# A second gate and up pair as seven products in seven of the FFNs, spread over the down stage

## The reference

```python
def swiglu(x, w_gate, w_up, w_down):
    return (jax.nn.silu(x @ w_gate) * (x @ w_up)) @ w_down
```

## Time and profile before

| | us |
|---|---|
| median of 3 runs | 2436.98 (2436.88 to 2441.23) |
| profiled execution | 2436.97 |
| its span | 2435.2 |
| PE busy | 2407.2 (99%), 12606 matmuls |
| VectorE busy | 1710.7 (70%) |
| ScalarE busy | 1255.4 (52%) |

### The profile page before, as it was taken

One profiled execution on the slowest core, in us unless ns is written; L12 is line 12 of the kernel. 1 busy time (PEld: TensorE's weight loads), 2 busy tenths in 40 slices (PEclk: granted clock), 3 DMA queues, 4 the chain that ended last, 5 costly groups with the idle time before them and its releaser, 6 DMA issues.

```text
span 2435.2 us, 30841 instructions
## 1 busy us (share of the span) xinstructions
PE 2407.2 (99%) x12606; PEld 2053.7 (84%) x12606; DVE 1710.7 (70%) x1755; ACT 1255.4 (52%) x1367; POOL 205.5 (8%) x358
## 2 busy tenths in 40 slices
PE   8999999999999999999999999999999999999998
PEld 6889998888889988888889878888888898778887
DVE  6555867857866778768658657777687677577884
ACT  5435545535537545445435664555455356645552
POOL 0100200101100100100100010001001000100010
PEclk9999999999999999999999999999999999999999
DMA  8765445856754446856864445468568544454672
GB/s 333 238 216 191 157 154 209 276 202 214 275 202 182 162 158 225 277 203 226 272 215 175 163 151 212 169 224 280 201 211 276 186 182 156 151 197 170 220 272 105
DMA packets 82549, 504.42 MB, mean 207 GB/s; under 512 B 11609, under 2 KB 12761, under 8 KB 30185
## 3 DMA queue, kind: packets, MB, share of 16 engines
q1 hardware_dynamic: 61488, 433.23, 49.4%
q0 software_dynamic: 19744, 67.65, 8.7%
q10 hardware_dynamic: 1176, 1.58, 0.4%
HBM read 476.72 MB, written 25.69 MB: 206 GB/s over the span
## 4 chain that ended last, share of the span: by engine, by line
PE 91%; DVE 5%; ACT 3%; issue 1%; DMA 1%; SPq 0%; POOL 0%; DVEq 0%; POOLq 0%; ACTq 0%
PE acc L709 23%; PE acc L711 22%; PE acc L710 22%; PE acc L677 4%; PE acc L678 4%; PE acc L679 4%; DVE w_lo L576 2%; PE aux L810 1%; PE aux L812 1%; PE aux L811 1%; PE aux L944 1%; ACT w_hi L568 1%; DMA raw<-in_w 1%; ACT tmp L1689 1%; PE bc L810 1%
## 5 line engine op out<-in xcount | busy, mean ns | idle before, releaser
L576 DVE TENSOR_TENSOR w_lo<-raw,w_hi 128x2048 fp32r<-128x2048 f32 (+1 forms) x438 | 978.7, 2245 | 489.1 <-ACT w_hi L568 487.9
L568 ACT ACTIVATE w_hi<-raw 128x2048 fp32r<-128x2048 f32 (+1 forms) x438 | 822.2, 1882 | 551.7 <-PE acc L711 387.6
L709 PE MATMUL acc<-w_hi,x_hi 128*128 128x512 f32 (+1 forms) x1624 | 633.4, 390 | 3.6 <-DVE x_lo L1941 2.1
L711 PE MATMUL acc<-w_lo,x_hi 128*128 128x512 f32 (+1 forms) x1624 | 628.5, 387 | 0.0
L710 PE MATMUL acc<-w_hi,x_lo 128*128 128x512 f32 (+1 forms) x1624 | 628.4, 387 | 0.0
L709 PEld LDWEIGHTS acc<-w_hi,x_hi 128*128 128x128 f32 x1624 | 305.0, 188 | 69.4 <-issue 6.1
L711 PEld LDWEIGHTS acc<-w_lo,x_hi 128*128 128x128 f32 x1624 | 305.0, 188 | 62.9
L710 PEld LDWEIGHTS acc<-w_hi,x_lo 128*128 128x128 f32 x1624 | 305.1, 188 | 61.7 <-issue 1.0
L709 PE MATMUL acc<-w_hi,h_parts 128*128 128x512 f32 x704 | 274.5, 390 | 0.0
L711 PE MATMUL acc<-w_lo,h_parts 128*128 128x512 f32 x704 | 274.0, 389 | 0.0
L710 PE MATMUL acc<-w_hi,h_parts 128*128 128x512 f32 x704 | 273.9, 389 | 0.0
(11 more groups left out here) (435 smaller groups left out, 2729.0 us busy)
## 6 DMA issues: line engine op xcount, KB each, us to landing
raw<-in_w SPq DMA_DIRECT2D x399, 1024.0 KB, 4.9
squares<-tmp POOLq DMA_DIRECT2D x40, 512.0 KB, 3.3
tmp<-squares POOLq DMA_DIRECT2D x160, 128.0 KB, 4.4
raw<-in_w SPq DMA_DIRECT2D x18, 512.0 KB, 4.8
tmp<-in_norm_gb POOLq DMA_DIRECT2D x8, 1024.0 KB, 5.9
tmp<-in_norm_gb POOLq DMA_DIRECT2D x6, 512.0 KB, 3.7
tmp<-in_gate_rows POOLq DMA_DIRECT2D x12, 256.0 KB, 2.9
squares<-tmp POOLq DMA_DIRECT2D x8, 256.0 KB, 2.8
```

What stands on the lines that cost most here:

```text
L568: nc.scalar.activation(w_hi[:, slot, 0:kind], raw[:, slots[c], 0:kind], ACT.Copy).then_inc(hi_done, 1)
L576: nc.vector.tensor_tensor(w_lo[:, slot, 0:kind], raw[:, slots[c], 0:kind], w_hi[:, slot, 0:kind].bitcast(F32), ALU.subtract).then_inc(lo_d ...
L709: nc.tensor.matmul(out, vh, wh, start=first and k == 0, stop=False)
L711: last = nc.tensor.matmul(out, vh, wl, start=False, stop=last_k and k == nk - 1)
```

## The change

In the seven FFNs behind the first sub-layer the block of 256 columns becomes block 4, and block 5 (now 512 columns) is computed with seven products as well. The first group starts at chunk 6 and has six plain chunks between its products in place of eight; its slots change (B22 is loaded into the slot of the chunk two before it). The second group starts at chunk 20. Its plain chunks are one of the block of 256 and five chunks of the down stage (blocks 0, 1, 2 for columns 0 to 511; blocks 0, 1 for columns 512 to 1023). Behind it come down chunks 33 to 39; block 5 is used in the last two, 38 and 39, and the last four chunks run tt = 0 first. Both groups use the same four input sums, for which other places in `h_parts` are taken. An FFN has 40 chunks in the stream, 6 of them sums, in place of 37 with 3. In `norm`, `add_out(s, 0, 1)` now stands behind `ahead.to(c + 2)` for these FFNs too, and `add_out(s, 0, 0)` directly ahead of `norm`. The weights are packed in the new order on the host. The core of the diff (lines that are only removed are left out in the functions that are printed above):

```diff
-FFN = [WIDE] * (UP_CHUNKS + 3 + 5) + [HALF] * 2 + [WIDE] * 5
+FFN = [WIDE] * 34 + [HALF] * 2 + [WIDE] * 4
 SUBS = ["ffn0", "mix1", "ffn"] + ["ffn", "mix1", "ffn"] + ["ffn", "mix2", "cross", "ffn"] * 2
 KINDS = {"ffn0": FFN0, "ffn": FFN, "mix1": MIX1, "mix2": MIX2, "cross": CROSS}
-TILES = {"ffn0": 26, "ffn": 22, "mix1": 30, "mix2": 46, "cross": 10}
+TILES = {"ffn0": 26, "ffn": 18, "mix1": 30, "mix2": 46, "cross": 10}
 B11, B21, B12, B22 = range(4)
-GROUP = (4 + B12, 0, 4 + B11, 1, 4 + B22, 2, None, 3, None, 8, 4 + B21, 9, None, 10, 11)
-G_T1, G_FORE, G_B11, G_FORE_GATE, G_B22, G_FORE2, G_T2, G_FORE_UP, G_T3, G_AFT, G_B21, G_AFT_GATE, G_T4, G_AFT2, G_AFT_UP = range(15)
-SLOT_OF = {G_B22: 3, G_FORE2: 2, G_T2: 6, G_FORE_UP: 3, G_T3: 6, G_B21: 3, G_AFT_GATE: 3, G_T4: 6}
-GROUP_AT = 8
+G_T1, G_B11, G_PLAIN0, G_PLAIN1, G_B22, G_PLAIN2, G_T2, G_PLAIN3, G_T3, G_PLAIN4, G_B21, G_PLAIN5, G_T4 = range(13)
+G_LEN, G_AFTER = 13, 14
+SLOT_OF = {G_B22: 2, G_PLAIN2: 2, G_T2: 6, G_PLAIN3: 3, G_T3: 7, G_B21: 3, G_PLAIN5: 3, G_T4: 6}
+GROUPS_AT = (6, 20)
...
+    def rows(n, at):
+        return turned_rows(down[at:at + 512, 512 * n:512 * n + 512])
+    (gate1, gate1_), (up1, up1_), (gate2, gate2_), (up2, up2_) = (block(w, at) for at in (512, 1024) for w in (gate, up))
+    half_ = moving(np.concatenate([gate[:, 2048:2304], up[:, 2048:2304]], 1))
+    b11, b21, b12, b22 = quarters(1536)
+    out[WIDE] += [*block(gate, 0), *block(up, 0), gate1, gate1_,
+                  b12, b11, up1, up1_, b22, gate2, gate2_, up2, b21, up2_, half_[:1]]
+    b11, b21, b12, b22 = quarters(2304)
+    out[WIDE] += [b12, b11, half_[1:], rows(0, 0), b22, rows(0, 512), rows(0, 1024), rows(1, 0), b21, rows(1, 512),
+                  rows(0, 1536), rows(1, 1024), rows(1, 1536), rows(0, 2304), rows(1, 2304)]
+    out[HALF] += [turned_rows(down[2048:2304, 512 * n:512 * n + 512]) for n in range(2)]
 def pack(i):
     out = {WIDE: [], HALF: [], LAT: []}
     for l in range(LAYERS):
         for f in (1, 2):
+            put = ffn_weights if l or f == 2 else first_ffn_weights
+            put(out, i[f"ffn{f}_w_gate"][l], i[f"ffn{f}_w_up"][l], i[f"ffn{f}_w_down"][l])
             if f == 1:
                 w = i["w_in"][l]
...
                 if c >= RING:
                     last = max(p for p in range(c) if slots[p] == slots[c])
                     sp.wait_ge(lo_done, last + 1)
-                    if c - G_FORE_UP in group_at:
-                        sp.wait_ge(weight_sum, 4 * group_at.index(c - G_FORE_UP) + 2)
-                    if c - G_AFT_UP in group_at:
-                        sp.wait_ge(weight_sum, 4 * group_at.index(c - G_AFT_UP) + 4)
+                    if c - G_PLAIN3 in group_at:
+                        sp.wait_ge(weight_sum, 4 * group_at.index(c - G_PLAIN3) + 2)
+                    if c - G_AFTER in group_at:
+                        sp.wait_ge(weight_sum, 4 * group_at.index(c - G_AFTER) + 4)
                 if c == 2:
                     sp.dma_start(flat(x), t["x"]).then_inc(x_and_ident_loaded, 16)
                     sp.dma_start(ident[:, :], t["ident"]).then_inc(x_and_ident_loaded, 16)
...
+                def group(g, b, plain):
                     a_, b_, e_ = aux[:, 0, :], aux[:, 1, :], bc[:, :]
                     x11, x12, _, x22 = ((x_hi[:, k, at], x_lo[:, k, at]) for k, at in X_AT)
                     s1, s3, s2, s4 = zip(SUM_HI, SUM_LO)
+                    pe.wait_ge(sum_parts, 4 * (f - 1) + 1)
                     if b:
                         pe.wait_ge(outs_ready, 3 * b - 2)
                     product(g + G_T1, e_, *s1, True)
                     if b:
                         pe.wait_ge(kept_silu, 2 * b)
                     product(g + G_B11, b_, *x11, True)
+                    plain(0, g + G_PLAIN0)
+                    plain(1, g + G_PLAIN1)
+                    pe.wait_ge(sum_parts, 4 * f)
                     pe.wait_ge(kept_copied, 3 * b + 1)
                     product(g + G_B22, e_, *s4, False)
+                    plain(2, g + G_PLAIN2)
                     pe.wait_ge(kept_copied, 3 * b + 2)
                     product(g + G_T2, b_, *s2, False)
+                    plain(3, g + G_PLAIN3)
                     pe.wait_ge(kept_copied, 3 * b + 3)
                     product(g + G_T3, b_, *s3, False)
+                    plain(4, g + G_PLAIN4)
                     if b:
                         pe.wait_ge(outs_ready, 3 * b)
                     product(g + G_B21, a_, *x12, True)
+                    plain(5, g + G_PLAIN5)
                     pe.wait_ge(outs_ready, 3 * b + 2)
                     product(g + G_T4, b_, *x22, False)
+                def down(c, n, q, first, last_k, tts=(0, 1)):
                     chunk_ready(c)
                     for tt in tts:
                         tile = tile_base[s + 1] - 4 + 2 * n + tt
                         if first:
                             bank_free(tile)
+                        if n == 0 or s == 0:
+                            pe.wait_ge(hid_parts, 12 * f + 2 * q + tt + 1)
+                        last = tokens(c, tile, tt, h_hi, h_lo, first_k(f, q), tiles_of(f, q), first, last_k)
                         if tt:
...
+                def half_and_downs(j, c):
+                    if j == 0:
+                        both(c, t0 + 12, 1)
+                    else:
+                        n, q = ((0, 0), (0, 1), (0, 2), (1, 0), (1, 1))[j - 1]
+                        down(c, n, q, q == 0, False)
+                if s:
+                    skewed_in(s, c0, t0)
+                    for j in range(2):
+                        both(c0 + 4 + j, t0 + 4, j)
+                    group(c0 + GROUPS_AT[0], 2 * (f - 1), gates_and_ups)
+                    if s == 6:
+                        bias_rows()
+                    both(c0 + 19, t0 + 12, 0)
+                    group(c0 + GROUPS_AT[1], 2 * (f - 1) + 1, half_and_downs)
+                    down(c0 + 33, 0, 3, False, False)
+                    down(c0 + 34, 0, 4, False, False)
+                    down(c0 + 35, 1, 4, False, False)
+                    for tt in range(2):
+                        down(c0 + 36, 1, 2, False, False, (tt,))
+                        down(c0 + 37, 1, 3, False, False, (tt,))
+                        down(c0 + 38, 0, 5, False, True, (tt,))
+                        if tt and parts(s + 1):
+                            x_turn(s + 1, 0)
+                        down(c0 + 39, 1, 5, False, True, (tt,))
+                    return
...
+                def first_group(g, b):
+                    ahead.to(g + 3)
                     silu(1, 0)
                     silu(1, 1)
                     ahead.to(g + 4)
+                    act.wait_ge(sum_parts, 4 * f)
+                    keep(g + G_T1, Q5B, bc[:, :])
+                    ahead.to(g + 5)
+                    keep(g + G_B11, P1B, aux[:, 1, :])
                     hid_high(0)
+                    ahead.to(g + 9)
+                    keep(g + G_T2, UB, aux[:, 1, :])
+                    ahead.to(g + 11)
                     silu(2, 0)
                     silu(2, 1)
                     ahead.to(g + 14)
                     act.wait_ge(outs_ready, 3 * b + 3)
                     nc.scalar.activation(P1B, P1B, ACT.Silu).then_inc(kept_silu, 1)
+                    ahead.to(g + 16)
+                    nc.scalar.activation(G1B, aux[:, 1, :], ACT.Silu).then_inc(kept_silu, 1)
+                    hid_high(1)
+                    if s == 6:
+                        bias_copy()
+                def second_group(g, b):
+                    ahead.to(g + 4)
+                    act.wait_ge(hid_ready, 12 * f + 8)
+                    keep(g + G_T1, Q5B, bc[:, :])
+                    ahead.to(g + 5)
+                    keep(g + G_B11, P1B, aux[:, 1, :])
+                    ahead.to(g + 6)
                     silu(4, 0)
                     silu(4, 1)
+                    ahead.to(g + 7)
                     hid_high(2)
+                    ahead.to(g + 8)
+                    hid_high(3)
+                    ahead.to(g + 9)
+                    keep(g + G_T2, UB, aux[:, 1, :])
+                    ahead.to(g + 11)
+                    hid_high(4)
+                    ahead.to(g + 14)
+                    act.wait_ge(outs_ready, 3 * b + 3)
+                    nc.scalar.activation(P1B, P1B, ACT.Silu).then_inc(kept_silu, 1)
                     ended_chunk(act, g + G_T4)
                     nc.scalar.activation(G1B, aux[:, 1, :], ACT.Silu).then_inc(kept_silu, 1)
+                    ahead.to(g + 17)
+                    choose_sqrt()
+                    ahead.to(g + 19)
+                    hid_high(5)
                     if s == 6:
+                        bias_store()
+                if s:
+                    silu(0, 0)
+                    whole(s, 1, 1)
+                    ahead.to(c0 + 4)
+                    silu(0, 1)
+                    ahead.to(c0 + 5)
+                    for q in range(4):
+                        sum_high(q)
```

(87 more changed lines are left out.)

212 lines of the change are left out of this document (67 added, 145 removed).

## The result

The changed kernel takes 2450.11 us (median of eight; 2444.4 to 2465.04) against 2436.98 (2436.88 to 2441.23): ratio 1.006, 95% interval 1.0045 to 1.0075. It is slower by 13 us; the forecast was 9 us faster.

The account below looks back on a forecast made before the run. PE, busy 99% of the span, was taken as the bound: number of matmuls times 0.227 us plus waits. 2437.0 - 19.0 (matmuls) + 6.1 (seams) + 3 (block 5) + 1 (first group) = 2428 us, range 2423 to 2441.

Parts of the forecast that it names:

- The matmuls: PE in seven FFNs: eight half-products become seven, 84 matmuls fewer in all, saving 19.0 us.
- The seam: Between sub-layers: add_out(s, 0, 1) moves onto the path, 0.70 us at three seams and 1.32 at three, 6.1 us.
- The first group: Products from chunk 6: least VectorE slack 1.9 us, chunk 11's transfer has 6.7 us; priced at 1 us over the kernel.
- the rival that it binds: VectorE and the slot two back bind in the first group: 1 to 2 us x 7, 2432 to 2438; chance 0.17.
- The rule wait = turn - 13.3 us: At chunk 38: PE waits for block 5 by what its transfers, from the transposes' start, take beyond 13.3 us.
- the size of block 5's turn: Block 5's store and loads before chunk 38: about as long as block 3's, costing 3 us, bounds 0 and 7 x 4.5.
- block 3's stretch: Time around block 3's store and loads in the kernel before, 11.0 to 14.1 us, taken as the model for block 5.
- block 5 waits as block 2 did: Rival at chunk 38: a turn of 15.2 us takes the gain, 15.9 gives 2442; chance 0.16, of it 0.10 above 2442.
- Costed at nothing: Second group: splits at least 4 us ahead, keeps and output sums too, all hidden by PE; cost nothing.
- The 9 us by the Trainium skill: Block 5's store and four loads at 2.0 us plus bytes at 436 GB/s: never waits; set aside for rows of 11 and more.
- The clock stays at its level: TensorE's granted clock stays 1.00, since PE gets busier rather than less; no cost counted.

Follow-up runs that it names:

- the span without a turn: Changed kernel with block 5 of the seven FFNs stored and loaded only as a 32-column sliver, the rest stale: 2426.45 us, ratio 0.9957.
- the hold: Changed kernel with SP waiting for block 5's landing before fetching the next sub-layer's first weight chunk: 2431.16 us, ratio 0.9976.
- two that gave nothing alone: Each against the changed kernel: add_out(s, 0, 1) ahead of the next sub-layer's first splits, 2452.17 us; block 5 turned in two token halves, 2450.34 us.
- the kernel with all three edits: Changed kernel with next weights held until block 5 lands, add_out(s, 0, 1) earlier, and block 5 turned by token halves: 2420.86 us, ratio 0.9936.

## Why the prediction was wrong

**Right.** The matmuls: 84 fewer, and the span without a turn, 2423.0, is 2435.2 - 19.0 + 6.1 = 2422.3 to 0.7 us. The seam: the stretch of 8.96 us became 9.66 and that of 9.46 became 10.76, so 0.70 and 1.30 at three seams each, 6.0 us against 6.1. (The listed waits are 0.26 and 1.36, forecast "near 0.7 and 1.8 us with the transposes' own"; and PE was idle for only 0.06 us where the prediction had it "waiting" before.) The first group: one wait of 0.2 us on a weight, against 1 us priced over the whole kernel, so the rival that it binds did not come true. The rule wait = turn - 13.3 us, to 0.1 in every case where the turn ended last.

**The step that failed** is the size of block 5's turn: "The load then is three weight chunks plus 1 MB of the turn within 13 us, about as in block 3's stretch, so I take 3 us; bounds 0 and 7 x 4.5." The 3 us were 25.5 in the profiled execution, six waits of 1.6 to 8.4 us; in the medians the turn with all that hangs on it costs 23.7. (25.5 lies inside the bounds; the range of the forecast did not reach so far.) The load is not that of block 3's stretch. The engines were at 0.99 for 21.7 us in sub-layer 5, which moved 6.5 MB of weights, six chunks; in the last FFN, with 2.0 MB beside it, the turn took at most 11.3 us. (A long turn also has more bytes in it; that the weights are the cause rests on the hold, which changed nothing else and took 28.7 us to 7.2.) The trace of before had a sign of it, in the two turns that the prediction read, of 11.6 and 17.8 us (DMA share and GB/s are the last two numbers):

```profile
468.87:480.49 11.62, 11.62 (x53) 9.63 (x52) 9.03 (x9) 3.89 (x4) 3.29 (x6) 1.00 0.89 297
1157.42:1175.25 17.83, 17.83 (x81) 14.75 (x80) 12.57 (x10) 7.24 (x6) 2.75 (x5) 1.00 0.96 310
```

I counted the chunks that PE uses up in 13 us and left out that SP, its slots free, fetches the next sub-layer's first ones just then. The upper bound per sub-layer (4.5, from block 2's longest turn of 17.8) was also too low: two turns were over 20. The rival "block 5 waits as block 2 did" had the sign and the wait, at 0.16, but neither the next sub-layer's weights nor the clock. A smaller term was missed beside it: the second group, "Costed at nothing", waited 3.2 us behind late weight chunks.

The 9 us by the Trainium skill (DMA: Bandwidth & Descriptors, "Anatomy of one DMA") was set aside rightly, but not far enough. The same page, section "Queues, rings and completion order", has the part that bears on it: each DMA engine serves the queues that have work in turn, a packet at a time. The rows fit that (share 0.99, the turn twice as long as with the engines at 0.76), though none shows the order of packets.

**The second failure** is "The clock stays at its level (1.00 in every stretch read)". I read stretches without a long pause in them; the longest wait before, after the first chunk, was 1.5 us. The waits cost 28.7 us, and of the 11.5 beyond them 9.8 are the clock. Without the falls the profiled execution would have stood near 2455, an estimate (2465.0 - 9.8). The Trainium skill (TensorE: Matmul & The Clock Gate, "HAM oscillation — how this bites in real kernels") warns of waits on DMA between bursts of matmuls; these rows agree, and add that such a pause need not come often: single ones of 3.3 us, and some of 1.8 to 2.5, were enough.

**Left open.** Why like turns differ (14.9 us in sub-layer 6, 21.7 in sub-layer 5), why the FFN's own last chunk lands later with the next weights held, and what decides on the clock in pauses of 1.8 to 4 us.

## What to carry to other kernels

When a result gets a new last dependency that goes through DRAM, count every byte that the prefetcher will have in flight then, the next stage's too, and not the bytes that the compute engine uses up in that time: a prefetch that runs ahead is free until something urgent shares its engines. Holding it for that one transfer gave 19 us here and made no new wait on the held weights. Look at the order of the engines too: a late transfer whose split stands ahead of the urgent work delays it, and the wait goes by the name of the urgent tile. Price a pause of TensorE of over 3 us at itself and 1.4 to 3 us of clock; and test the edits together, for two that gave nothing alone gave 4.5 and 6 us behind the third.

## What the hardware showed that I had not expected

- A single pause of 1.8 to 4 us in a stream of matmuls at 2.4 GHz can bring the granted clock to the 1.2 GHz level for 3 to 6 us, with the DMA engines idle or full alike. 22 of 25 pauses of over 3.2 us did, none of 35 of 1.3 to 1.7 did.
- In the two longest turns, with the DMA engines at 0.99 and 1.00, the store of 512 KB took 7.1 and 7.5 us and the last load behind it 11.0 and 9.4, where the medians from issue to landing over the whole kernel are 3.0 and 3.6 us.
- The changed kernel scatters by 20 us (2444.4 to 2465.04), the kernel with all three edits by 4 (2420.6 to 2424.82). In the profile of the first PE waits for block 5's turn in six sub-layers, and the turns vary from 14.9 to 21.7 us; in that of the second it never does.
